# Part of the first expert's input product for all tokens, placed among the routing steps of a two-layer decoder kernel

## The chip, the cores and the metric

One core of one Trainium2 chip runs the whole program. The metric is device time in microseconds (us): 1663.69 us is the median of three runs before the change (1661.57 to 1665.89).

## What is computed

Two decoder layers over 256 tokens of width 1024. Each layer has a mixer (a state-space part called S5, attention, and a gated delta rule), an output projection, a residual sum and a layer norm, and then a channel mixer with its own residual sum and norm. Layer 0's channel mixer is dense. Layer 1's is a mixture of eight experts of which each token uses two:

```python
def swiglu(x, w_gate, w_up, w_down):
    return (jax.nn.silu(x @ w_gate) * (x @ w_up)) @ w_down

def moe_ffn(x, router_w, w_gate, w_up, w_down):
    logits = (x @ router_w).astype(F32)
    top_val, top_idx = lax.top_k(logits, TOP_K)       # TOP_K = 2
    gates = jax.nn.softmax(top_val, axis=-1)
    ...
    for e in range(N_EXPERTS):                        # 8
        out = out + combine[..., e:e + 1] * swiglu(x, w_gate[e], w_up[e], w_down[e])
```

The hidden width is 3584. Everything is float32.

## The kernel before

**Pieces.** The channel mixers stream their weights in pieces of 128 x 2048 floats (1 MB). An expert has 42: for each of seven chunks `j` of 512 hidden columns two gate pieces ("G"), two up pieces ("U"), and two down pieces ("D", issued one chunk late). SP loads a piece into one of seven `raw` buffers. ScalarE copies it, rounded, into one of three `hi` buffers (`high_part`, L607), VectorE subtracts to get `lo` (`low_part`, L1008), and TensorE multiplies with the three products hi x hi, lo x hi and hi x lo: `inward` (L1405) for G and U, `outward` (L1416) for D, twelve 512-column matmuls for each piece and block of 128 tokens. SP reloads a `raw` buffer once its `lo` is made (`lo_ready`), and ScalarE refills a `hi` once its piece is used (`piece_used`). Each engine runs its queue strictly in the order written.

**An expert.** The dense mixer takes both blocks of 128 tokens. An expert takes one block: the rows that were routed to it, `xg`. After the G and U pieces of a chunk ScalarE applies Silu (L645), VectorE multiplies (L1046, giving `hh`), TensorE transposes `hh` (`turn`, L1478) and ScalarE and VectorE split the result into `hT_e` hi and lo (L634, L1038). Each expert is written as OPENING (the four pieces of chunk 0), ROUND (the rest, with the next expert's OPENING inside it, in a loop over seven experts) and LAST.

**The hand-over from mixer to experts in layer 1**, around which the change is made. After the mixer's output projection (L1730), VectorE normalises `x` block by block (L984 to L997, `norm(2 * l)`). TensorE transposes each block (L1368), ScalarE and VectorE copy it to `xT` (L813, L1280), and TensorE makes the router's logits (L1799, two instructions for each of eight tiles and each block). VectorE picks the two experts of each token (L1295 to L1308), TensorE counts positions (L1804 to L1808), VectorE makes the row numbers `row_of` (L1325, `rows_ready`). GpSimd scatters the 256 tokens twice to `xg_rows` in device memory (L585, four indirect DMAs) and then scales `x` (L589). When the four have landed, SP reads the first expert's 128 rows back (`xg_in`, L450) and goes on with the weight pieces 7 and up (L442), TensorE transposes the rows (L1397), ScalarE and VectorE split them into `xg` (L612, L1014), and `expert(first, OPENING)` begins. By then pieces 0 to 6 are in `raw`, and 0 to 2 are split too, since `high_part(0, 0..2)` and `low_part` ran under the mixer.

Layer 0's hand-over is alike but has no routing: there the transposed block is split at once into `xs` (L807 and L1268, `xs_low`), VectorE making the lo half between two steps of the second block's norm, and the first 24 products of block 0 run before block 1 is transposed.

Of the kernel before, what the change touches and what calls it, by code (L numbers as in the profile page):

```python
# [17 lines left out]
ALU = mybir.AluOpType  # L18
ACT = mybir.ActivationFunctionType
# [6 lines left out]
P = 128  # L26
# [122 lines left out]
def build(nc, x_in, w_in, w_out, consts, params, s5_b, glu_w, ln, wg, wu, wd, mg, mu, md, zeros, xg_rows, y_rows, out):  # L149
    ctx = ExitStack()  # L150
    with ctx:
# [101 lines left out]
        ye = arena[:, A_HT + 2048:A_HT + 2048 + D]  # L253
        xg_in = arena[:, A_XS:A_XS + D]
        y_in = arena[:, A_RAW:A_RAW + 4 * D].rearrange("p (b k d) -> p b k d", b=2, k=2)
# [71 lines left out]
        xg_psum, xg_hi, xg_lo = (sem(n) for n in ("xg_psum", "xg_hi", "xg_lo"))  # L327
        ye_ready, y_stored, y_all = sem("ye_ready"), sem("y_stored"), sem("y_all")
        y_gathered = [sem(f"y_gathered_{b}") for b in range(NB)]
        out_ready, out_stored = sem("out_ready"), sem("out_stored")  # L330
# [5 lines left out]

        def by_block(q):

            return ps[:, (4, 3, 0, 1)[q], :].rearrange("p (k t) -> p k t", k=4)

# [197 lines left out]
        def _(pool):  # L538
# [59 lines left out]
        def _(act):  # L598
# [63 lines left out]
            def experts(first):  # L662
                expert(first, OPENING, 0, True)
                with act.Fori(first, first + NE - 1) as i:
                    expert(i, ROUND, R0, True)
                expert(first + NE - 1, LAST, R0, False)

            for l in range(L):
# [129 lines left out]

                if l:
                    norm(2 * l)  # L800
                else:
                    for q in range(4):
                        b, k = q // 2, q % 2 * 4
                        if q % 2 == 0:
                            norm(0, (b,))
                        act.wait_ge(xt_psum, 4 * (n_x + 1) + q + 1)
                        af(xs_x[0][:, k:k + 4, b * P:(b + 1) * P], by_block(q), ACT.Copy).then_inc(xs_hi, 1)  # L807
                    channel_mixer()
                    norm(1)
            for b in range(NB):  # L810
                for q in range(4 - 2 * b):
                    act.wait_ge(xt_psum, 12 + 4 * b + q + 1)
                    af(xT[:, 2 * q:2 * q + 2, b * P:(b + 1) * P],  # L813
                       ps[:, (4, 3, 6, 7)[q], :].rearrange("p (k t) -> p k t", k=2)[:, :, b * P:(b + 1) * P],
                       ACT.Copy).then_inc(xt_act, 1)
# [16 lines left out]
        def _(dve):  # L832
# [223 lines left out]
            def experts(first):  # L1056
                expert(first, OPENING, 0, True)
                with dve.Fori(first, first + NE - 1) as i:
                    expert(i, ROUND, R0, True)
                expert(first + NE - 1, LAST, R0, False)  # L1060

            for l in range(L):
# [200 lines left out]
                def xs_low(b):  # L1263

                    for q in (2 * b, 2 * b + 1):
                        part = slice(q % 2 * 4, q % 2 * 4 + 4)
                        dve.wait_ge(xs_hi, q + 1)
                        tt(xs_x[1][:, part, b * P:(b + 1) * P], by_block(q),  # L1268
                           xs_x[0][:, part, b * P:(b + 1) * P].bitcast(F32), ALU.subtract).then_inc(xs_lo, 1)

                norm(2 * l, (0, 1, 2, 5), lambda q: dve.wait_ge(res_psum, 4 * l + q + 1),
                     (lambda: xs_low(0)) if l == 0 else None)
                if l == 0:
                    xs_low(1)
# [3 lines left out]
            for q in range(2, 4):  # L1278
                dve.wait_ge(xt_psum, 16 + q + 1)
                v_.tensor_copy(xT[:, 2 * q:2 * q + 2, P:T],  # L1280
                               ps[:, (4, 3, 6, 7)[q], :].rearrange("p (k t) -> p k t", k=2)[:, :, P:T])\
                    .then_inc(xt_dve, 1)
            def r8(a, n=16):
# [40 lines left out]
            step(ts(row_of[:, 0:2], m1, float(P * NE), None, ALU.add))  # L1324
            ts(row_of[:, 2:4], m2, float(P * NE), None, ALU.add).then_inc(rows_ready, 1)  # L1325
            step.wait()
# [22 lines left out]
        def _(pe):  # L1349
# [6 lines left out]
            def transpose_x(n, banks, blocks=range(NB)):  # L1356
                for b in blocks:
# [4 lines left out]
                    for k in range(KT):  # L1362
                        if n == 1:
                            dst = by_block(2 * b + k // 4)[:, k % 4, :]
# [4 lines left out]
                        if k % 4 == 3 if n == 1 else (b or n == 3) and k % 2:  # L1369
                            ins.then_inc(xt_psum, 1)  # L1370
# [136 lines left out]
            def experts(first):  # L1507
                expert(first, OPENING, 0, True)
# [282 lines left out]

            rw = par[:, PO["router"]:PO["router"] + KT * NE].rearrange("p (k e) -> p k e", k=KT)
            for b in range(NB):
                transpose_x(3, (4, 3, 6, 7), (b,))
                pe.wait_ge(xt_act, (8, 10)[b])
                if b:
                    pe.wait_ge(xt_dve, 6)
# [77 lines left out]
```

## Time and profile before

| | us |
|---|---|
| median of three runs | 1663.69 |
| the profiled execution, its own time | 1665.33 |
| its span in the trace | 1663.5 |
| TensorE busy | 1566.0 |
| VectorE busy | 1255.5 |
| ScalarE busy | 921.3 |
| mean granted TensorE clock | 0.974 |

PE is TensorE's matmul, PEld its weight loads, DVE is VectorE, ACT ScalarE, POOL GpSimd, SPq the DMA queue that SP issues to. PEclk is the granted TensorE clock, where 1.00 is 2.4 GHz and 0.50 is 1.2 GHz. All times count from the span's start. A row of the timeline gives the start, the time, the engine, the line and what it did, with the idle time before it in brackets.

### The profile page before, as it was taken

How to read it: one execution, taken by the hardware profiler on the slowest of the kernel's cores; microseconds unless marked ns; L12 is line 12 of the kernel's file. 1: busy time of each engine (PE TensorE's matmuls, PEld its weight loads, DVE VectorE, ACT ScalarE, POOL GpSimd, SP SyncE). 2: the span in 40 equal slices, each digit the busy share in tenths (PEclk: the TensorE clock that was granted, in tenths of full speed). 3: DMA queues.
4: the chain of work that ended last, by engine and by line, in shares of the span. 5: the costliest groups of instructions: out<-in, count | busy, mean ns of one | idle time of the engine just before them, and what ended most of it. 6: DMA issues, size and time to landing. Idle time of an engine off the chain costs nothing.

```text
span 1663.5 us, 22585 instructions
## 1 busy us (share of the span) xinstructions
PE 1566.0 (94%) x8706; PEld 1264.1 (76%) x8706; DVE 1255.5 (75%) x1164; ACT 921.3 (55%) x761; POOL 93.6 (6%) x123
## 2 busy tenths in 40 slices
PE   8998899999899994899999999999999999999992
PEld 7766488888777753688888888888888888888881
DVE  7984745444538754588888888888888888888884
ACT  1253143434104420577777777777777777777771
POOL 0010094000000201000000000000000000000000
PEclk9999999999999996799999999999999999999996
DMA  8694256554442204699999999999999999999972
GB/s 311 232 314 166 102 200 204 196 183 152 152 153 101 79 22 146 247 387 376 357 394 369 374 395 346 399 392 350 395 395 349 395 394 349 396 391 364 393 278 90
DMA packets 192882, 469.57 MB, mean 282 GB/s; under 512 B 7024, under 2 KB 11248, under 8 KB 192304
## 3 DMA queue, kind: packets, MB, share of 16 engines
q1 hardware_dynamic: 189360, 453.70, 74.5%
q0 software_dynamic: 2304, 10.77, 1.8%
q10 hardware_dynamic: 1152, 4.19, 0.6%
q8 instruction: 45, 0.74, 0.2%
q14 instruction: 21, 0.17, 0.0%
HBM read 461.29 MB, written 25.17 MB: 292 GB/s over the span
## 4 chain that ended last, share of the span: by engine, by line
issue 60%; PE 31%; DVE 6%; DMA 1%; ACT 1%; POOL 1%; POOLq 0%; SPq 0%; DVEq 0%
PE ps L1405 9%; PE ps L1378 6%; PE ps L1416 4%; PE ps L1730 2%; PE ps L1385 2%; PE ps L1668 1%; PE ps L1682 1%; PE ps L1678 1%; DVE arena L926 1%; DVE arena L944 1%; DVE small L985 1%; DMA arena<-in_w_in 1%; DVE x L993 0%; DVE x L997 0%; PE ps L1588 0%
## 5 line engine op out<-in xcount | busy, mean ns | idle before, releaser
L1008 DVE TENSOR_TENSOR lo<-arena,hi 128x2048 fp32r<-128x2048 f32 x378 | 869.3, 2304 | 223.5 <-ACT hi L607 222.9
L607 ACT ACTIVATE hi<-arena 128x2048 fp32r<-128x2048 f32 x378 | 723.3, 1919 | 358.2 <-PE ps L1405 231.2
L1405 PE MATMUL ps<-hi,xg 128*128 128x512 f32 x1792 | 557.5, 392 | 3.2 <-DVE xg L1014 2.6
L1405 PEld LDWEIGHTS ps<-hi,xg 128*128 128x128 f32 x1792 | 337.7, 189 | 76.0 <-DVE lo L1008 3.4
L1405 PE MATMUL ps<-lo,xg 128*128 128x512 f32 x896 | 350.5, 391 | 0.0
L1416 PE MATMUL ps<-hi,hTe 128*128 128x512 f32 x896 | 283.8, 398 | 2.2 <-DVE hTe L1038 2.2
L1405 PEld LDWEIGHTS ps<-lo,xg 128*128 128x128 f32 x896 | 169.5, 189 | 35.6
L1416 PEld LDWEIGHTS ps<-hi,hTe 128*128 128x128 f32 x896 | 164.8, 189 | 34.9 <-DVE lo L1008 2.6
L1416 PE MATMUL ps<-lo,hTe 128*128 128x512 f32 x448 | 175.8, 392 | 0.0
L1405 PE MATMUL ps<-hi,xs 128*128 128x512 f32 x448 | 139.2, 392 | 2.9 <-issue 2.9
L1378 PE MATMUL ps<-arena 128*128 128x256 f32 x544 | 123.6, 390 | 3.6 <-DMA arena<-in_w_in 2.4
L1378 PEld LDWEIGHTS ps<-arena 128*128 128x128 f32 x544 | 106.3, 196 | 21.1 <-issue 5.1
L1405 PEld LDWEIGHTS ps<-hi,xs 128*128 128x128 f32 x448 | 84.6, 190 | 20.6 <-issue 3.1
L1416 PEld LDWEIGHTS ps<-lo,hTe 128*128 128x128 f32 x448 | 84.5, 189 | 19.0
L1405 PE MATMUL ps<-lo,xs 128*128 128x512 f32 x224 | 87.6, 391 | 0.0
L686 ACT ACTIVATE arena<-ps 128x512 f32<-128x512 f32 (+2 forms) x26 | 14.2, 546 | 116.8 <-PE ps L1378 95.8
L1416 PE MATMUL ps<-hi,hTd 128*128 128x512 f32 x224 | 69.5, 391 | 0.0
L1730 PE MATMUL ps<-arena 128*128 128x512 f32 x128 | 58.1, 602 | 2.6 <-DVE arena L1206 2.6
L593 POOL DMA_INDIRECT arena<-y_rows,row_of x4 | 3.9, 964 | 972.5 <-DVE rt L1340 971.6
L1405 PEld LDWEIGHTS ps<-lo,xs 128*128 128x128 f32 x224 | 42.3, 189 | 8.8
L1416 PEld LDWEIGHTS ps<-hi,hTd 128*128 128x128 f32 x224 | 41.6, 188 | 8.3
L1730 PEld LDWEIGHTS ps<-arena 128*128 128x128 f32 x128 | 23.3, 190 | 29.2 <-issue 24.9
(318 smaller groups left out, 1279.4 us busy)
## 6 DMA issues: line engine op xcount, KB each, us to landing
arena<-in_mg SPq DMA_DIRECT2D x112, 1024.0 KB, 7.1
arena<-in_mu SPq DMA_DIRECT2D x112, 1024.0 KB, 7.2
arena<-in_md SPq DMA_DIRECT2D x112, 1024.0 KB, 7.0
arena<-in_w_in SPq DMA_DIRECT2D x7, 2048.0 KB, 9.4
arena<-in_wg SPq DMA_DIRECT2D x14, 1024.0 KB, 5.1
arena<-in_wu SPq DMA_DIRECT2D x14, 1024.0 KB, 5.2
arena<-in_wd SPq DMA_DIRECT2D x14, 1024.0 KB, 5.0
xg_rows<-in_zeros SPq DMA_DIRECT2D x1, 8704.0 KB, 35.8
```

What stands on the lines that cost most here:

```text
L607: af(hi[r % PARTS][:, :], raw[r % RAWS], ACT.Copy).then_inc(hi_ready, 1)
L926: ins = stt(qkv[:, c, :], cin[:, c, w:w + T], cw[:, c, w:w + 1], qkv[:, c, :], ALU.mult, ALU.add)
L944: ins = tt(turned_by, bu, table[:, two, :].unsqueeze(2).to_broadcast([P, 2, 2, T]), ALU.mult)
L985: step(v_.bn_stats(stats[:, 6 * c:6 * c + 6], xc))
L1008: tt(lo[r % PARTS][:, :], raw[r % RAWS], hi[r % PARTS][:, :].bitcast(F32), ALU.subtract)\
L1378: ins = mm(ps[:, bank, col:col + T], w[:, k, c0:c0 + P], xT[:, k, :], start=(k == 0), stop=(k == KT - 1))
L1385: ins = mm(ps[:, bank, 0:n], xT[:, k, b * P:(b + 1) * P], w[:, k, c0:c0 + n], start=(k == 0), stop=(k == KT - 1))
L1405: ins = mm(ps[:, (4 if w == "G" else 4 + nb) + b, :], tok[a][:, kk * nt + b * P:kk * nt + (b + 1) * P], tiles_of(part[r % PARTS], w)[:, k, ...
L1416: ins = mm(ps[:, 2 * b + c, :], hT[a][:, h0:h0 + P], tiles_of(part[r % PARTS], "D")[:, q, 512 * c:512 * (c + 1)], start=(j == 0 and p == 0 ...
L1668: ins = mm(ps[rows, (2, 5)[n % 2], c0:c0 + CH], M[(v + 1) % 2][rows, i, :], Tm[rows, i, :], start=True, stop=True)
L1678: mm(ps[rows, (1, 3, 6)[g], c0:c0 + CH], U[rows, i, :], A[rows, i, :], start=True, stop=True)
L1730: return mm(ps[:, (0, 1, 2, 5)[bank_at], :], xT[:, k, b * P:(b + 1) * P], wo[k // 4][:, k % 4, 512 * c:512 * (c + 1)], start=first, stop=f ...
```

## The change

Chunk 0 (pieces 0 to 3, 512 gate and 512 up columns) of the first expert is no longer multiplied with the 128 routed rows but with all 256 tokens. These 96 matmuls are spread over the hand-over: 12 between the transposes of block 0 and block 1, 12 behind the logits, 72 behind the counting of positions. For this `x` is also split into `xs` in layer 1, as in layer 0. The hidden values `hh` of both blocks are then multiplied with a 0/1 matrix `pick` (256 x 128, made by VectorE from the row numbers), which selects and transposes in one step, in place of `turn(0)`. `expert(0, OPENING)` goes away on all three engines. The splitting of pieces 3 to 6 moves ahead with it. `xg_in` gets another place, since `xs` now uses its old one.

```diff
-        def by_block(q):
-
-            return ps[:, (4, 3, 0, 1)[q], :].rearrange("p (k t) -> p k t", k=4)
+        def by_block(q, l=0):
+
+            return ps[:, q if l else (4, 3, 0, 1)[q], :].rearrange("p (k t) -> p k t", k=4)
...
-            pool.wait_ge(xt_psum, 20)
+            pool.wait_ge(xt_psum, 16)
...
             def experts(first):
-                expert(first, OPENING, 0, True)
+                if first:
+                    expert(first, OPENING, 0, True)
...
+                def row_copy(q):
+
+                    b, k = q // 2, q % 2 * 4
+                    act.wait_ge(xt_psum, 12 + q + 1)
+                    af(xT[:, k:k + 4, b * P:(b + 1) * P], by_block(q, 1), ACT.Copy).then_inc(xt_act, 1)
+
+                for q in range(4):
+                    b, k = q // 2, q % 2 * 4
+                    if q % 2 == 0:
+                        norm(2 * l, (b,))
+                    if l and q < 3:
+                        row_copy(q)
+                    elif l:
+                        act.wait_ge(xt_dve, 5)
+                    act.wait_ge(xt_psum, 4 * (n_x + 1) + q + 1)
+                    af(xs_x[0][:, k:k + 4, b * P:(b + 1) * P], by_block(q, l), ACT.Copy).then_inc(xs_hi, 1)
...
             af(rt[:, 100:102], rt[:, 98:100], ACT.Exp).then_inc(gate_exp, 1)
+            high_part(0, PARTS)
+            act.wait_ge(piece_used, NP + 2)
+            af(sg[:, :], ps[:, 4:6, :].rearrange("p a n -> p (a n)"), ACT.Silu).then_inc(gate_silu, 1)
+            high_part(0, PARTS + 1)
+            high_part(0, PARTS + 2)
             tokens_high(1)
+            high_part(0, PARTS + 3)
+            act.wait_ge(ht_psum, FC + 1)
+            af(hT_e[turned_in(0)][0][:, :], ps[:, 6, :], ACT.Copy).then_inc(ht_hi, 1)
             experts(0)
...
                 norm(2 * l, (0, 1, 2, 5), lambda q: dve.wait_ge(res_psum, 4 * l + q + 1),
-                     (lambda: xs_low(0)) if l == 0 else None)
+                     lambda: xs_low(0))
+                if l:
+                    dve.wait_ge(xt_psum, 16)
+                    v_.tensor_copy(xT[:, 4:8, P:T], by_block(3, 1)).then_inc(xt_dve, 1)
+                xs_low(1)
...
             ts(row_of[:, 2:4], m2, float(P * NE), None, ALU.add).then_inc(rows_ready, 1)
+            r1, r2 = rt[:, 110:112], rt[:, 112:114]
+            step(ts(r1, m1, float(P * NE), None, ALU.add))
+            step.then(ts(r2, m2, float(P * NE), None, ALU.add))
+            for b in range(NB):
+                step.then(ts(pick[:, b, :], C("iota"), r1[:, b:b + 1], None, ALU.is_equal))
+                ins = stt(pick[:, b, :], C("iota"), r2[:, b:b + 1], pick[:, b, :], ALU.is_equal, ALU.add)
...
             dve.wait_ge(route_ready, 1)
+            low_part(0, PARTS)
             most = dve.value_load(count_i[0:1, 0:1], min_val=0, max_val=T)
+            low_part(0, PARTS + 1)
+            dve.wait_ge(piece_used, NP + 4)
+            dve.wait_ge(gate_silu, FC + 1)
+            tt(hh[:, :], ps[:, 6:8, :].rearrange("p a n -> p (a n)"), sg[:, :], ALU.mult).then_inc(h_ready, 1)
+            low_part(0, PARTS + 2)
             tokens_low(1)
+            low_part(0, PARTS + 3)
+            dve.wait_ge(ht_hi, FC + 1)
+            tt(hT_e[turned_in(0)][1][:, :], ps[:, 6, :], hT_e[turned_in(0)][0][:, :].bitcast(F32), ALU.subtract)\
+                .then_inc(ht_lo, 1)
...
+            def first_inward(r, b):
+
+                pe.wait_ge(lo_ready, NP + r + 1)
+                pe.wait_ge(xs_lo, 4 + 2 * (b + 1))
+                return inward(*SEQ[r], r, b, NB, xs, T)
+
+            transpose_x(3, None, (0,))
+            first_inward(0, 0)
+            transpose_x(3, None, (1,))
+            pe.wait_ge(xs_lo, 4 + 2)
             for b in range(NB):
-                transpose_x(3, (4, 3, 6, 7), (b,))
-                pe.wait_ge(xt_act, (8, 10)[b])
+                pe.wait_ge(xt_act, (6, 7)[b])
...
             ins.then_inc(lg_psum, 1)
+            first_inward(1, 0)
             pe.wait_ge(sel_ready, 1)
...
+            first_inward(0, 1).then_inc(piece_used, 1)
+            first_inward(1, 1).then_inc(piece_used, 1)
+            for r in (2, 3):
+                first_inward(r, 0)
+                first_inward(r, 1).then_inc(piece_used, 1)
 
             tokens_turned(None, 16)
+            pe.wait_ge(h_ready, FC + 1)
+            pe.wait_ge(pick_ready, 1)
+            for q in range(4):
+                for b in range(NB):
+                    ins = mm(ps[:, 6, q * P:(q + 1) * P], hh[:, 512 * b + q * P:512 * b + (q + 1) * P], pick[:, b, :],
+                             start=(b == 0), stop=(b == 1))
+            ins.then_inc(ht_psum, 1)
+            pe.wait_ge(xg_hi, 1)
+            pe.wait_ge(xg_lo, 1)
             experts(0)
```

## Rows read from the trace of the kernel before

**Rows 1.** The page: busy time by engine.

```profile
PE 1566.0 (94%) x8706; PEld 1264.1 (76%) x8706; DVE 1255.5 (75%) x1164; ACT 921.3 (55%) x761; POOL 93.6 (6%) x123
```

**Rows 2.** Busy time in stretches: us from A:B, then us and (instructions) by engine.

```profile
640.00:669.50 29.50, 9.87 (x44) 8.92 (x44) 6.42 (x31) 3.28 (x5) 9.31 (x5) 0.50 0.48 179
...
1000.00:1200.00 200.00, 199.83 (x911) 164.76 (x910) 176.39 (x96) 149.53 (x102) 0.00 (x0) 1.00 1.00 376
```

**Rows 3.** Waits of TensorE's weight loads, 700 to 1640: total, times, longest.

```profile
PEld ps L1405 <- DVE lo L1008: 3.4, 7, 0.6
```

**Rows 4.** Waits of the SP queue, 720 to 1640.

```profile
SPq L442 <- DVE lo L1008: 619.5, 272, 4.7
```

**Rows 5.** Timeline, 628 to 700: start, us, engine, line, count.

```profile
632.88 1.09 PE L1368 MATMUL ps<-cst,x 128*128 128x128 f32 x8 [0.30 <-DVE x L997]
...
637.38 1.28 DVE L997 SCALAR_TENSOR_TENSOR x<-x,small,score_rows 128x1024 f32<-128x1024 f32 x1
...
646.25 0.17 DVE L1295 COPY rt<-ps 128x16 f32<-128x16 f32 x1 [3.74 <-PE ps L1799]
...
648.82 0.17 DVE L1308 TENSOR_TENSOR rt<-rt 128x16 f32<-128x16 f32 x1
...
652.75 0.16 DVE L1325 TENSOR_SCALAR row_of<-rt 128x2 uint32<-128x2 f32 x1
...
661.65 5.38 POOL L589 TENSOR_SCALAR x<-x 128x2048 f32<-128x2048 f32 x1 [3.01 <-DMA xg_rows<-x,row_of]
...
664.98 1.97 PE L1397 MATMUL ps<-cst,arena 128*128 128x128 f32 x8 [13.64 <-DMA arena<-xg_rows]
...
668.04 1.23 DVE L1014 TENSOR_TENSOR xg<-ps,xg 128x1024 fp32r<-128x1024 f32 x1 [14.67 <-ACT xg L612]
...
669.52 1.19 PE L1405 MATMUL ps<-hi,xg 128*128 128x512 f32 x2 [2.58 <-DVE xg L1014]
...
687.53 1.20 PE L1405 MATMUL ps<-hi,xg 128*128 128x512 f32 x2
```

**Rows 6.** Timeline of TensorE, 693 to 722: the first product of a down piece.

```profile
700.94 0.62 PE L1416 MATMUL ps<-hi,hTe 128*128 128x512 f32 x2
```

**Rows 7.** Chain of work in order of time: start, us, what, count.

```profile
297.27 21.76 PE ps L1405 x96
...
450.35 29.52 PE ps L1378 x128
```

**Rows 8.** Timeline of layer 0, 199 to 216, TensorE.

```profile
201.01 1.09 PE L1368 MATMUL ps<-cst,x 128*128 128x128 f32 x8 [0.30 <-DVE x L997]
205.01 1.19 PE L1405 MATMUL ps<-hi,xs 128*128 128x512 f32 x2 [2.91 <-issue]
...
211.94 1.03 PE L1368 MATMUL ps<-cst,x 128*128 128x128 f32 x8
```

**Rows 9.** Busy time in short stretches; the third number from the end is PEclk.

```profile
637.00:638.00 1.00, 0.70 (x7) 0.70 (x7) 0.93 (x3) 0.25 (x1) 0.00 (x0) 1.00 0.06 23
...
642.60:646.30 3.70, 3.55 (x16) 3.49 (x16) 0.05 (x1) 0.32 (x1) 0.00 (x0) 0.50 0.12 51
649.00:651.40 2.40, 2.30 (x10) 2.21 (x10) 0.50 (x3) 0.13 (x1) 0.00 (x0) 0.50 0.00 0
...
669.50:675.20 5.70, 5.68 (x13) 4.45 (x14) 0.00 (x0) 0.12 (x1) 0.00 (x0) 0.50 0.68 274
683.50:686.70 3.20, 0.00 (x0) 0.00 (x0) 2.88 (x3) 2.08 (x2) 0.00 (x0) 0.86 1.01 346
```

**Rows 10.** Timeline, 218 to 262, VectorE and GpSimd.

```profile
229.93 1.21 DVE L1025 TENSOR_TENSOR arena<-ps,arena 128x1024 f32<-128x1024 f32 x1
231.36 2.66 DVE L1008 TENSOR_TENSOR lo<-arena,hi 128x2048 fp32r<-128x2048 f32 x1 [0.23 <-ACT hi L607]
...
243.13 2.29 DVE L1008 TENSOR_TENSOR lo<-arena,hi 128x2048 fp32r<-128x2048 f32 x1 [2.03 <-ACT hi L607]
...
231.83 2.25 POOL L522 TENSOR_TENSOR s5s<-s5s 128x8 f32<-128x8 f32 x1
```

More of the change, by code:

```diff
@@ L253, in build @@
         ye = arena[:, A_HT + 2048:A_HT + 2048 + D]
-        xg_in = arena[:, A_XS:A_XS + D]
+        xg_in = arena[:, A_HT + 3072:A_HT + 3072 + D]
+        pick = score_rows[:, 2 * D:2 * D + T].rearrange("p (b s) -> p b s", b=2)
         y_in = arena[:, A_RAW:A_RAW + 4 * D].rearrange("p (b k d) -> p b k d", b=2, k=2)
@@ L328, in build @@
         ye_ready, y_stored, y_all = sem("ye_ready"), sem("y_stored"), sem("y_all")
+        pick_ready = sem("pick_ready")
         y_gathered = [sem(f"y_gathered_{b}") for b in range(NB)]
@@ L797, in norm @@
                             .then_inc(ln_std, 1)
[L799 to L807, printed above, removed]
+                def row_copy(q):
[12 more added lines that the diff above has]
+                    af(xs_x[0][:, k:k + 4, b * P:(b + 1) * P], by_block(q, l), ACT.Copy).then_inc(xs_hi, 1)
+                if l == 0:
                     channel_mixer()
                     norm(1)
[L810 to L815, printed above, removed]
             act.wait_ge(gate_exp_in, 1)
             af(rt[:, 100:102], rt[:, 98:100], ACT.Exp).then_inc(gate_exp, 1)
+            high_part(0, PARTS)
[3 more added lines that the diff above has]
+            high_part(0, PARTS + 2)
             tokens_high(1)
+            high_part(0, PARTS + 3)
+            act.wait_ge(ht_psum, FC + 1)
+            af(hT_e[turned_in(0)][0][:, :], ps[:, 6, :], ACT.Copy).then_inc(ht_hi, 1)
             experts(0)
@@ L1056, in experts @@
             def experts(first):
-                expert(first, OPENING, 0, True)
+                if first:
+                    expert(first, OPENING, 0, True)
                 with dve.Fori(first, first + NE - 1) as i:
@@ L1266, in xs_low @@
                         part = slice(q % 2 * 4, q % 2 * 4 + 4)
-                        dve.wait_ge(xs_hi, q + 1)
-                        tt(xs_x[1][:, part, b * P:(b + 1) * P], by_block(q),
+                        dve.wait_ge(xs_hi, 4 * l + q + 1)
+                        tt(xs_x[1][:, part, b * P:(b + 1) * P], by_block(q, l),
                            xs_x[0][:, part, b * P:(b + 1) * P].bitcast(F32), ALU.subtract).then_inc(xs_lo, 1)
                 norm(2 * l, (0, 1, 2, 5), lambda q: dve.wait_ge(res_psum, 4 * l + q + 1),
-                     (lambda: xs_low(0)) if l == 0 else None)
+                     lambda: xs_low(0))
[3 more added lines that the diff above has]
+                xs_low(1)
                 if l == 0:
-                    xs_low(1)
                     channel_mixer()
@@ L1277, in _ @@
                          dve.wait_ge(piece_used, NP))
[L1278 to L1282, printed above, removed]
             def r8(a, n=16):
@@ L1325, in _ @@
             ts(row_of[:, 2:4], m2, float(P * NE), None, ALU.add).then_inc(rows_ready, 1)
+            r1, r2 = rt[:, 110:112], rt[:, 112:114]
[4 more added lines that the diff above has]
+                ins = stt(pick[:, b, :], C("iota"), r2[:, b:b + 1], pick[:, b, :], ALU.is_equal, ALU.add)
+                if b:
+                    ins.then_inc(pick_ready, 1)
+                else:
+                    step(ins)
             step.wait()
@@ L1362, in transpose_x @@
                     for k in range(KT):
-                        if n == 1:
-                            dst = by_block(2 * b + k // 4)[:, k % 4, :]
+                        if n in (1, 3):
+                            dst = by_block(2 * b + k // 4, n // 3)[:, k % 4, :]
                         else:
@@ L1368, in transpose_x @@
                         ins = tr(dst, x[:, b, k * P:(k + 1) * P], ident)
-                        if k % 4 == 3 if n == 1 else (b or n == 3) and k % 2:
+                        if k % 4 == 3 if n in (1, 3) else b and k % 2:
                             ins.then_inc(xt_psum, 1)
@@ L1507, in experts @@
             def experts(first):
-                expert(first, OPENING, 0, True)
+                if first:
+                    expert(first, OPENING, 0, True)
                 with pe.Fori(first, first + NE - 1) as i:
@@ L1792, in _ @@
             rw = par[:, PO["router"]:PO["router"] + KT * NE].rearrange("p (k e) -> p k e", k=KT)
+            def first_inward(r, b):
[6 more added lines that the diff above has]
+            pe.wait_ge(xs_lo, 4 + 2)
             for b in range(NB):
-                transpose_x(3, (4, 3, 6, 7), (b,))
-                pe.wait_ge(xt_act, (8, 10)[b])
+                pe.wait_ge(xt_act, (6, 7)[b])
                 if b:
-                    pe.wait_ge(xt_dve, 6)
+                    pe.wait_ge(xt_dve, 5)
                 for k in range(KT):
```

## The prediction

> **What bounds the kernel now.** The page gives TensorE 94% of the span [rows 1], a mean over stages with different limits, so I read it stage by stage. In the expert loop TensorE sets the time: in 200 us it is busy 199.8 at full clock, VectorE 176.4 and ScalarE 149.5 [rows 2]. I then looked for waits in that loop. From 700 to 1640 the weight loads of the gate and up pieces waited for a `lo` seven times, 3.4 us in all [rows 3]. The weight stream isn't the bound: SP's queue spends 619.5 us waiting for buffers that VectorE must free [rows 4]. So the end of the kernel hangs on one moment, the one at which TensorE begins the loop's first piece (piece 4 of expert 0), and each microsecond that this comes earlier should be one at the end.
>
> In the hand-over before it TensorE works 9.87 of 29.5 us, at a clock of 0.50 [rows 2]. The timeline shows the chain: logits until 646.25, selection until 648.99, row numbers until 652.91, the scatter until GpSimd goes on at 661.65, the rows back in SBUF at 664.98, `xg` split at 669.27, first product at 669.52, and piece 4 at 687.53 [rows 5]. Only the four opening pieces, 48 matmuls, lie in the 18 us between the last two, with a stop of 3.2 us behind them [rows 9] while VectorE makes `hh`. The first down product starts at 700.94 [rows 6].
>
> **The unit prices.** 96 products take 21.76 us at full clock, 0.2267 each, 2.72 for twelve [rows 7]. At half clock 13 took 5.68 us, 0.437 each, before the clock came back at 675.2 [rows 9]. Piece 4 shows what a half-clock start costs: from 687.53 to 700.94 there are 48 products, 13.41 us against 10.88, so 2.5 us [rows 5 to 7].
>
> **What is added in front, step by step.** Layer 0 has the same beginning. Block 0's transposes stand at 201.01 there and at 632.88 here [rows 5, 8], 431.87 later.
>
> 1. The first 12 products. In layer 0 products begin at 205.01, behind the transposes, ScalarE's copies and VectorE's subtraction. 24 of them take 6.93 us, 1.5 more than at full clock [rows 7, 8]. Here then: begin at 636.9, and 12 take 2.72 + 1.5, until 641.1. Without a fall of the clock it would be 1.5 less.
> 2. VectorE puts two 512-column subtractions, together about the 1.23 of `xg` [rows 5], between the steps of block 1's norm. That norm was done at 637.38 + 1.28 = 638.7 and is now done at 639.9, still before 641.1. ScalarE's extra copies lie in time in which it has only the square roots to do. Transposes of block 1: 0.9, until 642.0.
> 3. Logits: 32 instructions. At full clock 7 took 0.70 us, 0.10 each; at half clock 16 took 3.55, 0.22 each [rows 9]. They come to 3.2 or 7.1 us. TensorE comes straight from products here, so I take full clock, 3.5 with the waits for copies: 645.5, against 646.25 before.
> 4. Selection, 648.99 − 646.25 = 2.8 us [rows 5]: 648.3. The 12 products of piece 1 fit in beside it (2.7).
> 5. Counting: 10 instructions, 2.3 us at half clock [rows 9], 1.1 at full: 649.5. Row numbers come 1.6 later, near 651.2, so the scatter starts 1.7 earlier than before and the rows are in SBUF at about 663.3 instead of 664.98.
> 6. The other 72 products: 72 x 0.2267 = 16.3, until 665.8. The rows have landed by then. The read of the first expert's rows, the scatter and the 13 us in which TensorE waited for them are thus covered by products, which is what the change lives on. `lo` of piece 3 is needed at 660.4. It can be made as soon as piece 0 is used (652.2), so it is in time.
>
> **What lies between the last product and piece 4.** VectorE must make `hh` of 1024 columns (1.21), then, because its queue is in order, `lo` of piece 5 (2.29), then `xg` (1.23) [rows 5, 10]: 4.7 and two hand-overs, 4.9 us, until 670.7. `lo` of piece 5 stands in front of `xg` though nobody needs it first. Beside this TensorE transposes the rows (0.9) and makes 16 instructions with 128 columns for `pick`. No row shows these. Below, they cannot be faster than the 0.10 of an 8-column one, and above, not slower than a 256-column one, 29.52 / 128 = 0.23 [rows 7, 9]: 1.6 to 3.7. Started at 667.2 they end at 668.8 to 670.9, hidden behind `xg` or nearly. The 64 products (fewer by 48, more by 96 and 16) cost nothing of their own, since all but the last stand in time that was idle. The `pick` instructions of VectorE, six small ones, stand behind `rows_ready` and delay only work that has slack.
>
> **The sum.** Piece 4 at 670.7 instead of 687.53 is 16.8 us. If it starts at full clock, its 2.5 us are saved too: 19.3 us.
>
> **What the clock takes of that.** After the last products the clock stood at 1.00 at 683.5 and at 0.50 by 687, having been at 0.86 on average between, with TensorE idle [rows 9]. During the logits of before it stayed at 0.50 though TensorE was busy 3.55 of 3.70 us [rows 9]. It rose in both openings only after a stretch of products. Two places of the new order hold work of that lighter kind for 4.5 to 5 us: transposes and logits (641 to 645.5), and rows, `pick` and the wait for `xg` (665.8 to 670.7). A fall in the first makes half the logits, piece 1's 12 products and part of the counting slow: 0.9 + 2.4 + 0.2, about 3.5 us. A fall in the second costs the 2.5 us of rows 5 to 7 again. I take one of the two, 3.0: 19.3 − 3.0 = 16.3 us. The profiled execution took 1665.33 around a span of 1663.5, the median is 1663.69, so I subtract from the median: 1647.4, rounded to 1647.5.
>
> **VectorE and GpSimd.** Where the two run side by side the trace shows them in each other's way: an eight-column GpSimd operation took 2.25 us beside a `lo`, and that `lo` took 2.66 instead of 2.29 [rows 10]. VectorE's `hh`-like operation, with one operand in PSUM, kept its 1.21. In the new order `lo` of piece 3 (about 654 to 656.5) falls among GpSimd's four scatters, and `lo` of piece 4 meets GpSimd's scaling of `x`, 5.38 us long [rows 5]. A scatter held up by one `lo` lands 2.3 later, at 665.6, just before TensorE asks. The Trainium skill (SBUF — State Buffer, "SBUF: two separate sides") goes further: the port pair is an exclusive lock, and a VectorE operation that holds it keeps GpSimd from writing descriptors at all. By the rows alone I charge nothing; by that rule the scatter would be later by whatever VectorE runs there. No row of before shows a scatter beside VectorE work.
>
> **The rivals.**
>
> - *Both falls of the clock* (or none). 19.3 − 6.0 = 13.3: 1650.4. None: 1644.4. For both: each stretch is longer than the stop in which the clock fell near 686. Against: in front of each lie products at full clock. Both 25%, none 12%.
> - *GpSimd and VectorE hold each other up so that the hand-over is late.* If `x`'s scaling goes first, `lo` of piece 4 waits for up to 5.4 us and `hh` behind it; if the scatter is held up more than once, TensorE waits for the rows behind its 96 products. 2 to 5 us on top of one fall: 1649.5 to 1652.5. For: rows 10. Against: 2.4 us of slack in front of the rows. 10%. The skill's lock is this rival's case.
> - *The weight stream is the bound after all.* SP still waits for the scatter before it loads piece 7, so the stream starts only 1.7 us earlier; if it set the end, that would be the gain: 1662. Against: rows 4. 4%, no measurable change.
> - *Slower: the clock does not come back among the opening products.* They are spread between lighter steps. All at half clock from 636.9: 12 x 0.437 + 2.0 + 7.1 + 5.2 + 2.3 + 72 x 0.437 + 4.9, which is 58.3 us, so piece 4 starts at 695.2, 7.7 later than before: 1671.4. It decides from about 39 us at half clock on, as each costs half a microsecond of the 19.3. Against: in layer 0 a loss of 1.5 us means that the clock was back after about 3 us of products, and at 675.2 it was back after 5.7. 3%.
>
> One fall is the forecast, 43%, with a range of its own from 1645.5 to 1649.5. Some 3% is left for what I don't see. Differences within 0.3% (5 us) can't be told from no change. Faster by more than that, below 1658.7: 43 + 25 + 12 + 10 and most of the rest, 92%; same 5%; slower 3%. The range holds none and both falls and the middle of the late hand-over: 1644 to 1653.
>
> **What would show it.** Right: TensorE's 96 products with `xs` lie between about 637 and 666, at full clock from 650 on at the latest; `row_of` is written near 651 to 654; the first product with `xg` near 671 to 674, and the first down product 10.9 to 13.4 us behind it; the loop afterwards has the same length as before. Wrong: TensorE waiting for the rows behind its opening products; an `lo` of 5 us or more beside GpSimd; waits for `lo` in the first round of the loop; or a longer loop, which would say that something else than TensorE's start sets the end.

## The result, and the profile after

Before and after ran in turns on one chip, four times each: 1663.23 us (1661.57 to 1665.89) before and 1648.11 us (1646.46 to 1648.95) after, a ratio of 0.991 with a 95% interval from 0.9896 to 0.9925. The change saves 15.1 us; the forecast was 1647.5. The profiled execution of after took 1648.54 us around a span of 1646.7. Lines have moved: `inward` L1405 is now L1436, `outward` L1416 is L1447, the transposes L1368 are L1399, the logits L1799 are L1841, `low_part` L1008 is L1020, the scatter L585 is L587.

The page of after, busy time and granted clock, to set beside [rows 1]:

```profile
PE 1569.6 (95%) x8766; PEld 1266.7 (77%) x8766; DVE 1257.5 (76%) x1173; ACT 923.0 (56%) x762; POOL 95.6 (6%) x123
...
PEclk9999999999999999999999999999999999999996
```

TensorE works 3.6 us more than before in a span 16.8 shorter. The timeline of after shows where, to set beside [rows 5, 6]:

```profile
635.26 1.09 PE L1399 MATMUL ps<-cst,x 128*128 128x128 f32 x8 [0.30 <-DVE x L1009]
639.30 1.19 PE L1436 MATMUL ps<-hi,xs 128*128 128x512 f32 x2 [2.95 <-DVE xs L1281]
643.57 1.04 PE L1399 MATMUL ps<-cst,x 128*128 128x128 f32 x8
644.44 3.64 PE L1841 MATMUL ps<-par,arena 128*128 128x8 f32 x32
647.93 0.71 PE L1436 MATMUL ps<-hi,xs 128*128 128x512 f32 x2
652.11 0.43 PE L1847 MATMUL ps<-rt,cst 128*128 128x8 f32 x2
653.38 0.72 PE L1436 MATMUL ps<-hi,xs 128*128 128x512 f32 x2
654.94 0.17 DVE L1336 TENSOR_SCALAR row_of<-rt 128x2 uint32<-128x2 f32 x1
657.39 0.97 POOL L587 DMA_INDIRECT xg_rows<-x,row_of  x1 [0.30 <-issue]
658.48 2.29 DVE L1020 TENSOR_TENSOR lo<-arena,hi 128x2048 fp32r<-128x2048 f32 x1 [1.68 <-ACT hi L609]
658.66 2.94 POOL L587 DMA_INDIRECT xg_rows<-x,row_of  x1 [0.30 <-issue]
665.32 0.34 SPq L452 DMA_DIRECT2D arena<-xg_rows  x1
669.81 1.04 PE L1428 MATMUL ps<-cst,arena 128*128 128x128 f32 x8
670.01 1.22 DVE L1357 TENSOR_TENSOR arena<-ps,arena 128x1024 f32<-128x1024 f32 x1 [5.17 <-PE ps L1436]
671.15 2.28 DVE L1020 TENSOR_TENSOR lo<-arena,hi 128x2048 fp32r<-128x2048 f32 x1
671.29 2.05 PE L1863 MATMUL ps<-score_rows,arena 128*128 128x128 f32 x16 [0.44 <-DVE arena L1357]
673.35 1.22 DVE L1026 TENSOR_TENSOR xg<-ps,xg 128x1024 fp32r<-128x1024 f32 x1
675.05 0.73 PE L1436 MATMUL ps<-hi,xg 128*128 128x512 f32 x2 [1.71 <-DVE xg L1026]
686.08 0.62 PE L1447 MATMUL ps<-hi,hTe 128*128 128x512 f32 x2
```

I count from block 0's transposes, since everything ahead of them varies between executions. The first down product comes 686.08 − 635.26 = 50.82 us behind them, where it was 700.94 − 632.88 = 68.06: the hand-over is 17.24 us shorter. It began 2.38 later in this execution, and what follows the first down product took 1646.7 − 686.08 = 960.6 instead of 1663.5 − 700.94 = 962.6. So 17.24 − 2.38 + 1.94 = 16.8, the difference of the spans. TensorE doesn't wait for the rows any more: they are transposed at 669.81, right behind the last of the 96 products. No 13.64 us of idle time stand in front of that row as they did in [rows 5].

The granted clock of after in short stretches (third number from the end), and the loop:

```profile
639.00:640.00 1.00, 0.70 (x2) 0.63 (x3) 0.96 (x3) 0.29 (x1) 0.00 (x0) 0.50 0.40 154
...
647.00:649.50 2.50, 2.50 (x16) 2.25 (x16) 1.18 (x7) 0.33 (x1) 0.00 (x0) 0.94 0.00 0
649.50:652.50 3.00, 3.00 (x10) 2.36 (x8) 1.64 (x11) 0.20 (x1) 0.00 (x0) 0.50 0.00 0
653.40:669.80 16.40, 16.40 (x74) 13.53 (x74) 7.42 (x19) 7.94 (x5) 10.28 (x5) 1.00 0.48 180
669.80:675.00 5.20, 3.10 (x25) 2.65 (x23) 4.99 (x4) 3.31 (x3) 1.05 (x1) 1.00 0.94 345
...
1000.00:1200.00 200.00, 199.83 (x911) 164.78 (x910) 176.57 (x96) 150.01 (x100) 0.00 (x0) 1.00 1.00 376
```

The clock is at 1.2 GHz twice, when the first products begin and again under piece 1's products, which follow 3.5 us of logits. It is at 2.4 GHz for the 72 products and stays there over the gap ahead of `xg`. The loop's row is that of [rows 2]. The waits of TensorE's weight loads behind the hand-over are unchanged too, to set beside [rows 3]:

```profile
PEld ps L1436 <- DVE lo L1020: 3.4, 7, 0.6
```

### The profile page after: what moved, and what is told of

It reads as the page before. It is cut to its first block, busy times and chain, and to the rows that moved or that the text cites. A ratio compares the mean times of both kernels' runs of the same rounds, so it can differ in the third digit from the quotient of the medians.

```text
span 1646.7 us, 22723 instructions
## 1 busy us (share of the span) xinstructions
PE 1569.6 (95%) x8766; PEld 1266.7 (77%) x8766; DVE 1257.5 (76%) x1173; ACT 923.0 (56%) x762; POOL 95.6 (6%) x123
## 4 chain that ended last, share of the span: by engine, by line
issue 59%; PE 31%; DVE 6%; DMA 1%; ACT 1%; POOL 1%; POOLq 0%; SPq 0%; DVEq 0%
PE ps L1436 10%; PE ps L1409 6%; PE ps L1447 4%; PE ps L1762 2%; PE ps L1416 2%; PE ps L1700 1%; PE ps L1714 1%; PE ps L1710 1%; DVE arena L938 1%; DMA arena<-in_w_in 1%; DVE arena L956 1%; DVE small L997 1%; DVE x L1005 0%; DVE x L1009 0%; PE ps L1620 0%
## 5 line engine op out<-in xcount | busy, mean ns | idle before, releaser
L1020 DVE TENSOR_TENSOR lo<-arena,hi 128x2048 fp32r<-128x2048 f32 x378 | 867.2, 2299 | 216.0 <-ACT hi L609 215.3
L1436 PE MATMUL ps<-hi,xg 128*128 128x512 f32 x1760 | 543.6, 390 | 2.3 <-DVE xg L1026 1.7
L1436 PEld LDWEIGHTS ps<-hi,xg 128*128 128x128 f32 x1760 | 329.1, 188 | 73.0 <-DVE lo L1020 3.4
L1436 PE MATMUL ps<-lo,xg 128*128 128x512 f32 x880 | 342.5, 389 | 0.0
L1447 PE MATMUL ps<-hi,hTe 128*128 128x512 f32 x896 | 282.6, 397 | 2.2 <-DVE hTe L1050 2.2
L1436 PEld LDWEIGHTS ps<-lo,xg 128*128 128x128 f32 x880 | 165.2, 188 | 34.5
L1447 PEld LDWEIGHTS ps<-hi,hTe 128*128 128x128 f32 x896 | 164.0, 188 | 34.6 <-DVE lo L1020 2.6
L1447 PE MATMUL ps<-lo,hTe 128*128 128x512 f32 x448 | 175.1, 391 | 0.0
L1436 PE MATMUL ps<-hi,xs 128*128 128x512 f32 x512 | 161.5, 397 | 5.9 <-DVE xs L1281 2.9
L1436 PEld LDWEIGHTS ps<-hi,xs 128*128 128x128 f32 x512 | 97.7, 192 | 26.5 <-issue 6.3
L1436 PE MATMUL ps<-lo,xs 128*128 128x512 f32 x256 | 101.4, 396 | 0.0
L1447 PEld LDWEIGHTS ps<-lo,hTe 128*128 128x128 f32 x448 | 84.2, 188 | 18.9
L1447 PE MATMUL ps<-hi,hTd 128*128 128x512 f32 x224 | 69.5, 391 | 0.0
L1436 PEld LDWEIGHTS ps<-lo,xs 128*128 128x128 f32 x256 | 49.0, 192 | 10.4
L1447 PEld LDWEIGHTS ps<-hi,hTd 128*128 128x128 f32 x224 | 41.6, 188 | 8.3
```

What stands on the lines that cost most here:

```text
L1020: tt(lo[r % PARTS][:, :], raw[r % RAWS], hi[r % PARTS][:, :].bitcast(F32), ALU.subtract)\
L1436: ins = mm(ps[:, (4 if w == "G" else 4 + nb) + b, :], tok[a][:, kk * nt + b * P:kk * nt + (b + 1) * P], tiles_of(part[r % PARTS], w)[:, k, ...
L1447: ins = mm(ps[:, 2 * b + c, :], hT[a][:, h0:h0 + P], tiles_of(part[r % PARTS], "D")[:, q, 512 * c:512 * (c + 1)], start=(j == 0 and p == 0 ...
```

## The experiments

Twelve runs. Those up to `e3` shared one set of runs of the kernel before (1662.84 us), `e4` to `e6` a second (1663.68), the last four timed ones a third (1663.28). Ratios below are against these. `e4` to `e6` ran on another chip than the rest, and the changed kernel did not run beside them, so they are compared with it through the kernel before. In most of the expectations Theory A is the prediction's account: TensorE's own work and VectorE's `hh`, `lo`, `xg` set the hand-over, and the clock takes some of it.

### The changed kernel again, twice

No edit.

> The changed kernel once more, beside the others of this group. Both theories: about 1648 us; its first product with xg about 39.8 us after block 0's transposes begin, as in its profile (675.05 against 635.26).

1648.18 us, ratio 0.9914 (0.99 to 0.9927). In its profile the clock fell once, at the first products; the first down product stands 682.67 − 633.09 = 49.58 us behind block 0's transposes. The first product with `xg` stands 671.65 − 633.09 = 38.56 behind them, 1.2 less than expected, since the second fall is missing.

> The changed kernel again, beside the others of this group: 1648 us. Its granted clock is expected to fall once or twice between block 0's transposes and the counting of positions.

1648.55 us, 0.9914 (0.9898 to 0.9929). Its profile, same rows as above:

```profile
635.77 1.09 PE L1399 MATMUL ps<-cst,x 128*128 128x128 f32 x8 [0.30 <-DVE x L1009]
...
672.88 0.73 PE L1436 MATMUL ps<-hi,xg 128*128 128x512 f32 x2 [1.68 <-DVE xg L1026]
683.88 0.61 PE L1447 MATMUL ps<-hi,hTe 128*128 128x512 f32 x2
```

This is 48.11 us, with a granted clock of 1.00 from 633 to 681. I had expected one fall or two, so this was a miss. The same program thus has its hand-over in 48.11, 49.58 or 50.82 us as the clock falls never, once or twice. A comparison of single profiles needs the clock's windows beside it.

### `xg` ahead of a `lo` that nobody awaits

```diff
+            tokens_low(1)
             low_part(0, PARTS + 2)
-            tokens_low(1)
             low_part(0, PARTS + 3)
```

> Only VectorE's order changes: the lo half of xg is made before the lo half of piece 5. Theory A (VectorE's queue order between the last opening product and piece 4 sets the start of the loop): xg is split at about 673.1 instead of 674.6, TensorE is then held only by the pick products that end at 673.3, so piece 4 starts 1.6 us earlier, 1646.5 us. Theory B (that gap is set by something else, or TensorE then waits for the lo of piece 5): no change, 1648.1, with a wait for lo in the first round.

1646.1 us (1644.41 to 1647.52), 0.9898 (0.9882 to 0.9913):

```profile
668.62 1.04 PE L1428 MATMUL ps<-cst,arena 128*128 128x128 f32 x8
670.10 2.05 PE L1863 MATMUL ps<-score_rows,arena 128*128 128x128 f32 x16 [0.44 <-DVE arena L1357]
670.75 1.23 DVE L1026 TENSOR_TENSOR xg<-ps,xg 128x1024 fp32r<-128x1024 f32 x1 [0.70 <-ACT xg L614]
...
672.42 0.72 PE L1436 MATMUL ps<-hi,xg 128*128 128x512 f32 x2 [0.28 <-issue]
```

From the end of the 96 products to the first `xg` product it is now 3.80 us instead of 5.24. The idle time ahead of that product was 1.68 us, ended by VectorE's `xg`; it is 0.28, ended by nothing but issue. So the `lo` in front of `xg` cost 1.4 us and not its whole 2.3, because VectorE now waits 0.70 us for ScalarE's half of `xg`. What bounds the gap after that isn't shown: the `pick` products end at 672.15 and the split at 671.98, and the first product follows the split by 0.44 us, as it does in the control (671.21 to 671.65). The median is 2.1 lower than the control's, of which these 1.4 are shown in the rows; the intervals of the two overlap.

### `lo` of piece 3 behind the scatter

GpSimd sets a semaphore behind its four scatters, with a write of one spare column, and VectorE waits for it.

```diff
+            pool.memset(rt[:, 150:151], 0.0).then_inc(scatter_issued, 1)
...
             dve.wait_ge(route_ready, 1)
+            dve.wait_ge(scatter_issued, 1)
             low_part(0, PARTS)
```

> VectorE makes the lo half of piece 3 only when GpSimd has issued all four scatters (a small GpSimd memset behind them gives the signal). Theory A (GpSimd's third scatter took 2.94 us instead of 0.97 because of that lo, but the rows still land about 1 us before TensorE asks for them): all four scatters take 0.95 to 1.1 us, the rows are read back 2 us earlier, and the time stays at 1648.1. Theory B (the delay of the scatter reaches the end): 1646.1. If the lo of piece 3 becomes late, TensorE waits for it before product 49 of the opening and the time rises.

1646.43 us (1645.1 to 1650.03), 0.9905 (0.989 to 0.9921):

```profile
655.72 0.95 POOL L588 DMA_INDIRECT xg_rows<-x,row_of  x1 [0.31 <-issue]
...
658.13 4.49 DVE L1022 TENSOR_TENSOR lo<-arena,hi 128x2048 fp32r<-128x2048 f32 x2 [4.27 <-POOL rt L590]
660.79 0.34 SPq L453 DMA_DIRECT2D arena<-xg_rows  x1
```

The third scatter takes 0.95 us instead of 2.92 to 2.98, and SP reads the rows 8.79 us behind `row_of` where the control's profile has 10.35. The first down product stands 49.57 behind block 0's transposes, the control's 49.58, and both profiles have the one fall of the clock at the first products. The delay by VectorE is real, and in the profile it is hidden, as Theory A says. The time alone wouldn't show this: the median, 1646.43, lies at Theory B's 1646.1 and not at Theory A's 1648.1, but its interval and the control's overlap, and `e7` below finds nothing more from the same edit.

### That `lo` made twice

`lo` of piece 3 is computed once more just ahead of its turn, into the same place.

```diff
+            dve.wait_ge(hi_ready, NP + PARTS + 1)
+            step(tt(lo[0][:, :], raw[PARTS], hi[0][:, :].bitcast(F32), ALU.subtract))
+            step.wait()
             low_part(0, PARTS)
```

> VectorE makes the lo half of piece 3 twice in a row (the first result is overwritten by the same values), so that VectorE works beside the scatters for 4.6 instead of 2.3 us. Theory A (GpSimd's descriptor work stops while VectorE runs such an operation; about 1 us of slack in front of the rows): a second scatter is held up by some 2 us, TensorE waits about 1 us for the rows, 1649.3 us, and the lo of piece 3 and 4 come later without being waited for. Theory B (only a single stall, or the slack is larger): 1648.1.

1649.82 us (1646.71 to 1650.66), 0.9918 (0.9904 to 0.9933), not distinguishable from the control:

```profile
659.41 2.95 POOL L587 DMA_INDIRECT xg_rows<-x,row_of  x1 [0.31 <-issue]
...
662.66 2.02 POOL L587 DMA_INDIRECT xg_rows<-x,row_of  x1 [0.30 <-issue]
667.02 0.34 SPq L452 DMA_DIRECT2D arena<-xg_rows  x1
...
670.57 1.04 PE L1431 MATMUL ps<-cst,arena 128*128 128x128 f32 x8
```

Now two scatters are held up, 2.95 and 2.02 us, and the read comes 11.33 us behind `row_of`. The row of the transposes still shows no idle time: in the kernel before the rows were there 666.11 − 662.74 = 3.37 us behind the read's issue, which gives 670.39 here, 0.2 us early. The wait that I looked for didn't appear, though the median lies near the 1649.3 that it was to give. The profile has both falls of the clock, which give this run its long hand-over (53.65), as in `e1`'s profile (52.18).

### The first 24 products moved

In the first kernel all 24 products that stand among transposes, logits and selection go behind the counting; in the second piece 1's twelve go in front, with piece 0's.

```diff
             transpose_x(3, None, (0,))
-            first_inward(0, 0)
             transpose_x(3, None, (1,))
...
-            first_inward(1, 0)
             pe.wait_ge(sel_ready, 1)
...
-            first_inward(0, 1).then_inc(piece_used, 1)
-            first_inward(1, 1).then_inc(piece_used, 1)
-            for r in (2, 3):
+            for r in range(4):
                 first_inward(r, 0)
                 first_inward(r, 1).then_inc(piece_used, 1)
```

> The 12 products between the transposes and the 12 beside the selection move behind the counting of positions, so that all 96 stand there in one row. Theory A (the 24 fill idle time and also hold the clock up for transposes, logits and counting): the routing steps run at half clock as in the kernel before, row numbers come 1 to 2 us later, the opening ends about 10 us later, 1658 us. Theory B (they only fill idle time): 24 x 0.2267 = 5.4 us later, 1653.5. Theory C (they delay the routing as much as they save): 1648.

1657.93 us (1656.91 to 1661.83), 0.9972 (0.9961 to 0.9982), as Theory A had it:

```profile
642.88 1.97 PE L1399 MATMUL ps<-cst,x 128*128 128x128 f32 x8 [5.82 <-DVE x L1009]
644.64 6.83 PE L1840 MATMUL ps<-par,arena 128*128 128x8 f32 x32
654.30 0.59 PE L1845 MATMUL ps<-rt,cst 128*128 128x8 f32 x2 [2.82 <-DVE rt L1319]
...
685.39 0.72 PE L1436 MATMUL ps<-hi,xg 128*128 128x512 f32 x2 [1.68 <-DVE xg L1026]
```

Without products in the early steps TensorE is at 1.2 GHz from 640 to 660: the transposes take 1.97 us and not 1.04, the logits 6.83 and not 3.64. The 24 products come on top of the 72 behind them. The median is some 9.6 us above the changed kernel's: 5.4 are the 24 products at full clock, and the rest, some 4 us, is what the slower steps ahead cost. (The profiled execution was the slowest of the ten, 1661.83.)

```diff
             transpose_x(3, None, (0,))
             first_inward(0, 0)
+            first_inward(1, 0)
             transpose_x(3, None, (1,))
...
-            first_inward(1, 0)
             pe.wait_ge(sel_ready, 1)
```

> Piece 1's 12 products of block 0 move from beside the selection to before block 1's transposes, as layer 0 has them. Theory A (beside the selection they are almost free even at half clock): logits end 2.7 us later, TensorE idles 2.8 us during the selection, the opening ends 1.2 to 2.5 us later, 1649.3 to 1650.6. Theory B (24 products in a row keep the clock up through logits and counting and so pay for it): 1648 or less.

1652.94 us (1650.2 to 1653.62), 0.9931 (0.9907 to 0.9955), 2.3 us above the upper end of what I had expected:

```profile
652.65 0.60 PE L1847 MATMUL ps<-rt,cst 128*128 128x8 f32 x2 [2.82 <-DVE rt L1319]
...
650.00:655.00 5.00, 2.35 (x11) 2.35 (x12) 2.68 (x17) 0.20 (x1) 0.00 (x0) 0.50 0.01 3
655.00:660.00 5.00, 5.00 (x13) 3.90 (x14) 2.82 (x17) 0.00 (x0) 2.07 (x2) 0.53 0.19 78
```

The selection is bare again, 2.82 us of idle time. The clock falls at 649.4, just before the logits end, and is back only near 659.6: counting and the first 11 of the 72 products go at half speed. It also fell at the first products, and the hand-over is 689.76 − 633.04 = 56.72 us. The profile of `e3`, which also has two falls, had 53.65, so the place of the twelve products is worth some 3 us. By the times alone this isn't beyond the intervals: the changed kernel's ratio is 0.9914 with 0.99 to 0.9927.

### The 72 products behind the rows

```diff
+            tokens_turned(None, 16)
             first_inward(0, 1).then_inc(piece_used, 1)
             first_inward(1, 1).then_inc(piece_used, 1)
             for r in (2, 3):
                 first_inward(r, 0)
                 first_inward(r, 1).then_inc(piece_used, 1)
-            tokens_turned(None, 16)
```

> The 72 products behind the counting move behind the transposes of the rows that come back from the scatter, so that nothing covers scatter and read. Theory A (the gain is the overlap of products with that round trip): TensorE is idle for some 13 us, runs cold afterwards, and piece 4 starts about 16 us later, 1664 us, the time of the kernel before. Theory B (the gain comes from the dropped stop behind the opening and from the clock at piece 4): most of it stays, below 1655.

1664.1 us (1662.76 to 1670.99), 1.0008 (0.9995 to 1.0021), as Theory A had it:

```profile
663.78 1.97 PE L1428 MATMUL ps<-cst,arena 128*128 128x128 f32 x8 [13.46 <-DMA arena<-xg_rows]
...
688.27 0.72 PE L1436 MATMUL ps<-hi,xg 128*128 128x512 f32 x2 [1.68 <-DVE xg L1026]
```

The 13.46 us of waiting for the rows are back, and the whole gain is gone: without products that cover the scatter and the read there is none. This doesn't make the early 24 worthless, since `e4` lost 9.6 us of the 15 with the cover in place. The two losses add up to more than the gain because the changed kernel makes 96 opening products and not 48. The 48 more are 10.9 us at 0.2267, and idle time has to take them before anything is gained.

### Both VectorE edits together

The edits of `e1` and `e2`.

> VectorE splits xg before piece 5, and makes the lo half of piece 3 only behind the issued scatters: both edits together. Theory A (only the first is on the path, worth 1.4 us between the last opening product and piece 4, as its profile showed: 3.80 us instead of 5.2): 1646.6, as with the first alone. Theory B (an earlier scatter is worth something of its own, as the lower median of that run hints): below 1645.5.

1646.4 us (1645.56 to 1650.19), 0.99 (0.9886 to 0.9914): no more than `e1` alone gives, as Theory A had it.

### TensorE kept busy while it waits for `xs`

Twelve 512-column products of `hi` of piece 0 with itself, whose result nobody reads, fill the 2.95 us ahead of the first product; the second kernel has `e1`'s edit as well.

```diff
             transpose_x(3, None, (0,))
+            pe.wait_ge(lo_ready, NP + 1)
+            for k in range(12):
+                mm(ps[:, 7, :], hi[0][:, 0:P], hi[0][:, 0:512], start=True, stop=True)
             first_inward(0, 0)
```

> Twelve matmuls of 512 columns, whose results nobody reads, stand in front of the first opening product, where TensorE waits 2.95 us for VectorE's first xs half. Theory A (that wait brings the clock down, and the half-clock products behind it cost 1.5 us or more, and a second fall behind the logits 1.4 us or more): no fall near 637 to 640, the first 12 products take 2.7 us, block 1's transposes begin 6.9 us behind block 0's instead of 8.3 to 9.3, 1645 to 1646.5 us. Theory B (the clock falls anyway because of the light work around, or at another place): 1648. Theory C (they outlast the wait and delay the opening): 1649.

1646.68 us (1645.55 to 1647.73), 0.9895 (0.988 to 0.991), just above Theory A's 1645 to 1646.5 and not clear of the change alone, run beside it. Block 1's transposes begin 6.91 us behind block 0's, as Theory A had it, but in the unfilled profile of `c1` it is 6.90. The profile, by stretches:

```profile
634.00:646.00 12.00, 11.52 (x74) 9.69 (x74) 9.22 (x14) 5.33 (x9) 0.57 (x1) 1.00 0.51 174
646.00:650.00 4.00, 4.00 (x12) 3.14 (x12) 2.82 (x17) 0.20 (x1) 0.00 (x0) 0.57 0.02 6
```

> The twelve filling matmuls and the earlier split of xg together. Theory A (the two act at different places of TensorE's path and add up): about 1.4 us below the filling alone, 1643.6 to 1645. Theory B: no faster than the better of the two alone.

1644.94 us (1639.89 to 1647.21), 0.9885 (0.9867 to 0.9902):

```profile
634.00:680.00 46.00, 44.97 (x235) 37.59 (x236) 31.00 (x57) 22.81 (x22) 11.93 (x6) 1.00 0.62 229
...
680.81 0.62 PE L1447 MATMUL ps<-hi,hTe 128*128 128x512 f32 x2
```

The fall at the first products is absent in both profiles; the one behind the logits came in `e8` and not in `e9`. But the first fall was absent in three unfilled profiles too (`c1`, `e5`, `e7`), so that the filling prevents it is not shown. The last kernel has the lowest median of all, 18.3 us below the kernel before; the first down product stands 46.71 us behind block 0's transposes. The time lies in Theory A's range, 1.7 us below `e8`, but the intervals of the two overlap. Against the change alone, run beside it, the 3.6 us are not fully beyond the intervals (0.9885 with 0.9867 to 0.9902, 0.9914 with 0.9898 to 0.9929).

### The kernel before, profiled again

No edit, one run.

> The kernel before the change, unaltered, profiled a second time. The first profile of it took 1665.33 us, some 2 us above its median of all runs (1663.2 to 1663.7), and it is the only one. The question is which part of it varies. In the first profile block 0 was transposed at 632.88 and the first down product came 68.06 us later; the changed kernel's profiles have 48.11 to 50.82 there and transpose block 0 between 631.2 and 636.0. Theory A (the hand-over of the kernel before varies with the granted clock as that of the changed one does): block 0's transposes between 631 and 636, the first down product 65.5 to 68.5 us later, and the rest of the span 960.5 to 963 us as in all profiles so far; own time within 3 us of 1663.5. Theory B (the change makes the part ahead of the hand-over longer): block 0's transposes at 633 or earlier again, and the hand-over 68 us again, so that the changed kernel's later start of 1 to 2 us on average is a cost of the change. One profile can weaken B, not prove it.

1663.13 us:

```profile
633.47 1.09 PE L1368 MATMUL ps<-cst,x 128*128 128x128 f32 x8 [0.30 <-DVE x L997]
...
670.65 1.19 PE L1405 MATMUL ps<-hi,xg 128*128 128x512 f32 x2 [2.57 <-DVE xg L1014]
...
687.08 0.71 PE L1405 MATMUL ps<-hi,xg 128*128 128x512 f32 x2
...
699.67 0.62 PE L1416 MATMUL ps<-hi,hTe 128*128 128x512 f32 x2
```

The hand-over is 66.20 us here, against 68.06. The opening takes 16.43 us instead of 18.01, piece 4 to the down product 12.59 instead of 13.41 [rows 5, 6]. What follows takes 1661.3 − 699.67 = 961.6. The kernel before varies as the changed one does.

## Why the prediction was right, point by point

1. **The mechanism.** One moment sets the end: the stretch behind the first down product is 960.6 to 962.8 us in the profiles of before, after and both controls. The gain is made where the prediction put it, by covering the scatter and the read; `e5` takes the cover away and the gain goes with it; `e4` takes the 24 early products away and two thirds of it go. Counted from block 0's transposes, the signs named for "right" came, the last of the 96 products 1.4 us behind the 666. The page counts 8766 − 8706 = 60 more TensorE instructions and not the 64 of the prediction, which forgot the four of `turn(0)`; that changes nothing in the sum.
2. **The first products** begin 4.04 us behind block 0's transposes (4.02 from layer 0), and 12 take 643.57 − 639.30 = 4.27 with the half-clock start (4.2). In the profile without a fall the second transposes come 1.4 us earlier, which is the 1.5 that was priced.
3. **Logits** 3.49 us to the next product (3.5). Piece 1's products took 4.18 instead of 2.7, since the clock fell beside them. **Counting** 1.27 (1.1, its start still slow). **The 72 products** 16.43 (16.3). **The gap** 5.24 (4.9). The `pick` products take 0.13 us each, inside the bounds 0.10 and 0.23, and are hidden: they end at 673.34, and `xg` is split only at 674.57.
4. **The first `xg` product** stands 39.79 us behind the transposes. The prediction had 670.7 − 632.9 = 37.8 at full clock, with 3.5 more for a fall in the first place. The fall was in the first place and cost 1.4, because it came only under piece 1's products and was over after 3 us. The other 0.6 are the small overruns of point 3.
5. **The second place** never had one: in all twelve profiles with the 96 products the mean clock is 1.00 from their last to the first down product, which stands 11.03 behind the first `xg` product in after (10.9). The forecast's 3.0 us for one fall was the mean of the two places; only the first has borne it, at half of that. The row that suggested it, 3.2 us of idle TensorE behind the opening [rows 9], had nothing in it; here rows and `pick` products fill 3.1 of 5.2.
6. **The size.** The hand-over has 67.1 us on average in two profiles of before and 49.5 in three of after, 17.6 less; the prediction took 16.3 from the median, and the medians differ by 15.1, 14.7 and 14.7. The two profiles of before were 0.9 us slower on average than its median, and the three of after began the hand-over 1.5 later on average (634.7 against 633.2). Twelve profiles with the changed start, all kernels together, have it between 631.25 and 635.98, around both of before, so I take that for scatter; a cost of the change of some 1.5 us ahead of the hand-over isn't excluded. That the forecast of 1647.5 is only 0.6 us from 1648.11 is luck in part. The clock term was 1.6 us too large (3.0 for 1.4) and the small terms 0.7 too small, so the sum should have been 17.2, which is what the profile shows, and not 16.3. The median gained 2.1 less than 17.2, for the reasons just given, so two errors of opposite sign leave 1.2. Half of that went because the forecast was subtracted from 1663.69, the median of three runs, which a fourth brought to 1663.23.
7. **The rivals.** GpSimd and VectorE do meet: the third scatter lies beside a `lo` of 2.29 us and takes 2.94 instead of 0.95. That is the 2.3 us that the prediction put at one `lo`, inside its slack. The Trainium skill (SBUF — State Buffer, "SBUF: two separate sides") has VectorE holding an exclusive lock that keeps GpSimd from writing descriptors; the rows agree, the scatter being longer by nearly the `lo`, and `e2` undoes it. With two such operations (`e3`) TensorE still didn't wait for the rows, but only 0.2 us were left. The other half of the rival, a `lo` beside GpSimd's scaling of `x`, didn't occur in after, where the second `lo` ends at 664.84 and the scaling begins at 665.46. It did in `e6`, where the `lo` took 4.85 us (its row stands in the last section). That is 2.6 us more than alone, about half of the 5.4 that the rival allowed, and the gap behind the last product stays at 5.24 there. The stream was no bound, and the clock came back in every profile.

## What to carry to other kernels

Work with no dependence on a chain of small steps was best spread between its steps, not put behind it (`e4`, 9.6 us more) or twelve products further in front (`e6`, 4 to 5 us more, not clear of the intervals): it fills the waits, and the small TensorE steps run at the higher clock. Put the operation that the next engine awaits ahead of one that nobody awaits yet, even when both are short: in a queue that runs in order that is worth up to the length of the other, here 1.4 of 2.3 us, because the operation then waits for another engine. Before a single profile's difference of a few microseconds is explained, profile the same kernel again.

## What the runs showed of the hardware

The granted clock isn't a fixed function of the program. One and the same kernel had no fall, one and two in three executions, 48.11 to 50.82 us for its hand-over, and where a fall is long (0.50 for 6.5 us at a stretch, twice, in `e1`) it is 52.18 with the later steps even shorter. In the profile of after, TensorE was near the end of 2.95 us of idle time when the clock fell first (at 639.0), and before the second fall it had run 8-column matmuls for 3.5 us and then 1.6 us of full ones. In `c1` it did the same work with the same idle time and kept 1.00, so neither is shown to be the cause.

An indirect scatter of 128 rows costs GpSimd 0.95 to 1.1 us, and 2.92 to 2.98 when it begins just behind a float32 subtraction of 128 x 2048 with both operands in SBUF. The subtraction keeps its 2.29. A scatter that was within 0.3 us of its end when the subtraction began kept its 0.95 (after, 661.91).

GpSimd's scaling of 128 x 2048 takes 5.38 to 5.40 us alone and 6.96 where a subtraction had begun before it (`e2`, `e7`); there it is the scaling that waits. Where the scaling had begun 0.9 us earlier, the subtraction took 4.85 and ended 0.4 us behind the scaling. Where it had begun 5.0 us earlier, the subtraction kept its 2.29, though the scaling's record ran on for 1.3 us (`e4`). From `e6`:

```profile
666.24 4.85 DVE L1020 TENSOR_TENSOR lo<-arena,hi 128x2048 fp32r<-128x2048 f32 x1 [1.78 <-ACT hi L609]
```
